# The first eight depth tiles of every down product as seven block products

## The reference

```python
def swiglu(x, w_gu, w_down):
    g, u = jnp.split(x @ w_gu, 2, axis=-1)
    return (jax.nn.silu(g) * u) @ w_down
...
x = layer_norm_2(DN_ALPHA * x + 0.5 * swiglu(x, ffn_w_gu[layer, 0], ffn_w_down[layer, 0]),
                 ln_g[layer, 0], ln_b[layer, 0])
```

## Time and profile before

| | |
|---|---|
| median of 3 runs | 2902.07 us (2901.93 to 2903.99) |
| profiled execution, its own time | 2903.62 us |
| its span, first to last instruction | 2901.8 us |
| TensorE busy | 2857.2 us, 98% of the span |
| DVE / ACT busy | 1707.7 us / 1269.3 us |
| mean granted clock of TensorE | 0.998 |

### The profile page before, as it was taken

One profiled execution on the slowest core, in us unless ns is written; L12 is line 12 of the kernel. 1 busy time (PEld: TensorE's weight loads), 2 busy tenths in 40 slices (PEclk: granted clock), 3 DMA queues, 4 the chain that ended last, 5 costly groups with the idle time before them and its releaser, 6 DMA issues.

```text
span 2901.8 us, 43274 instructions
## 1 busy us (share of the span) xinstructions
PE 2857.2 (98%) x18236; PEld 2507.2 (86%) x18236; DVE 1707.7 (59%) x2268; ACT 1269.3 (44%) x2082; POOL 101.5 (3%) x153
## 2 busy tenths in 40 slices
PE   8999999999999999999999999999999999999998
PEld 6888888778888699998868999898998886799987
DVE  4464342343333778862676988257884458698843
ACT  3324333454434345542473555134553248545531
POOL 1000000001000000000100000010000011000000
PEclk9999999999999999999999999999999999999999
DMA  6432232222222232333302233243333340123232
GB/s 200 141 105 88 102 102 87 88 67 81 80 88 80 71 102 93 112 117 107 100 16 88 91 113 117 91 129 131 108 97 116 79 110 1 59 88 117 88 116 73
DMA packets 186274, 278.67 MB, mean 96 GB/s; under 512 B 29595, under 2 KB 127051, under 8 KB 185953
## 3 DMA queue, kind: packets, MB, share of 16 engines
q1 hardware_dynamic: 177040, 247.17, 26.4%
q0 software_dynamic: 9040, 28.73, 3.1%
HBM read 271.56 MB, written 4.25 MB: 95 GB/s over the span
## 4 chain that ended last, share of the span: by engine, by line
PE 88%; DVE 7%; issue 2%; DMA 1%; ACT 1%; POOL 0%; SPq 0%; POOLq 0%; DVEq 0%; ACTq 0%
PE bank L673 25%; PE bank L675 25%; PE bank L674 25%; PE bank L811 2%; PE bank L899 1%; PE bank L867 1%; PE bank L883 1%; PE bank L831 1%; PE bank L820 1%; PE bank L684 1%; PE bank L687 1%; PE bank L686 1%; PE bank L792 1%; DMA raw<-in_ffn_w_gu 1%; PE bank L1049 0%
## 5 line engine op out<-in xcount | busy, mean ns | idle before, releaser
L1932 DVE TENSOR_TENSOR w_low<-raw,w_high 128x2048 fp32r<-128x2048 f32 (+2 forms) x131 | 293.7, 2242 | 663.3 <-ACT w_high L1463 657.0
L1463 ACT ACTIVATE w_high<-raw 128x2048 fp32r<-128x2048 f32 (+2 forms) x131 | 245.3, 1873 | 527.5 <-PE bank L675 525.6
L673 PE MATMUL bank<-xt_high,w_high 128*128 128x512 f32 (+1 forms) x1128 | 407.2, 361 | 1.3 <-DVE w_low L1932 0.8
L675 PE MATMUL bank<-xt_high,w_low 128*128 128x512 f32 (+1 forms) x1128 | 399.1, 354 | 0.0
L674 PE MATMUL bank<-xt_low,w_high 128*128 128x512 f32 (+1 forms) x1128 | 398.5, 353 | 0.0
L673 PE MATMUL bank<-w_high,hidden_high 128*128 128x512 f32 x640 | 249.3, 390 | 0.0
L675 PE MATMUL bank<-w_high,hidden_low 128*128 128x512 f32 x640 | 249.0, 389 | 0.0
L674 PE MATMUL bank<-w_low,hidden_high 128*128 128x512 f32 x640 | 249.0, 389 | 0.0
L673 PEld LDWEIGHTS bank<-xt_high,w_high 128*128 128x128 f32 x1128 | 212.8, 189 | 38.3 <-issue 9.6
L675 PEld LDWEIGHTS bank<-xt_high,w_low 128*128 128x128 f32 x1128 | 212.8, 189 | 31.0
L674 PEld LDWEIGHTS bank<-xt_low,w_high 128*128 128x128 f32 x1128 | 213.1, 189 | 27.3
(11 more groups left out here) (447 smaller groups left out, 7096.0 us busy)
## 6 DMA issues: line engine op xcount, KB each, us to landing
raw<-in_ffn_w_gu SPq DMA_DIRECT2D x80, 1024.0 KB, 5.2
raw<-in_ffn_w_down SPq DMA_DIRECT2D x44, 1024.0 KB, 4.9
raw<-in_b_w_in SPq DMA_DIRECT2D x40, 1024.0 KB, 5.1
raw<-in_a_w_in SPq DMA_DIRECT2D x23, 1024.0 KB, 5.1
raw<-in_a_w_out SPq DMA_DIRECT2D x8, 1024.0 KB, 4.9
raw<-in_ffn_w_gu SPq DMA_DIRECT2D x16, 512.0 KB, 5.4
raw<-in_w_out SPq DMA_DIRECT2D x5, 1024.0 KB, 4.9
raw<-in_w_mem_kv SPq DMA_DIRECT2D x4, 1024.0 KB, 5.2
```

Source lines behind the costliest of these rows:

```text
L673: pe.matmul(o, lh, rh, start=start, stop=False, skip_group_check=True)
L675: return pe.matmul(o, ll, rh, start=False, stop=stop, skip_group_check=True)
L1463: act.activation(homes[n][0][:, 0:w], RAW[n % 2][:, 0:w], ACT.Copy).then_inc(sem["w_high_ready"], step("w_high_ready", n))
L1932: dve.tensor_tensor(homes[n][1][:, 0:w], RAW[n % 2][:, 0:w], homes[n][0][:, 0:w].bitcast(F32), ALU.subtract).then_inc(sem["w_low_ready"], ...
```

## The change

With the tokens in two halves, the depth tiles 0 to 7 in two halves of four, and the output columns in two halves of 512, the part of the down product that belongs to the first eight depth tiles is a 2 x 2 by 2 x 2 block product. Before, it is done as four panels with all eight block products. After the change it is done as seven block products, numbered b = 0 to 6, of 24 matmuls of 512 columns each (two token tiles, four depth tiles, three matmuls each). Their left operands are hidden blocks or sums of them, their right operands weight blocks or differences of them:

- `block_sum(1)` to `(4)` on DVE make the token sums, in `SUMS`, three buffers of 4 KB a partition. The first three are made in units 5, 6 and 7, behind n = 2; they are split into parts beside the last unit. The space comes from the scratch of GpSimd's transfers, `dynamic_dma_scratch_size`, which goes from 16 KB to 4 KB.
- The four weight blocks of 512 x 512 are loaded as three panels and a fourth, `CORNER`, that lies where the gains of the layer norms lie; GpSimd's next load of gains waits until the corner has been used. `block_difference(1)` to `(4)` on DVE make the weight differences, in the raw buffers or in `LATE` (where the snapshots of the units lie).
- `block_high(b)` on ACT and `block_low(b)` on DVE split the weight operand of each block product into the same two rings.
- Several block products add up in one bank. Where an intermediate result belongs to an output of its own, `add_partial` on DVE adds it from the bank to the residual rows `X`, and TensorE waits for that (`partial_added`) before it adds the next block product to the same bank.
- The ring's order is now: blocks 0 to 3, the panel of depth tiles 8 and 9, block 4, the panel of 10 and 11, blocks 5 and 6, and the other panels as before.

The core of the diff:

```diff
+        for name, k0, c0 in (("block", 0, 0), ("block", 0, 512), ("down", 8, None), ("block", 4, 0)):
...
+        for k0 in range(10, KF, 2):
+            add(("down", l, i), [(0, 2, D, D, rows(wd, k0, 2, 0, D))])
...
+            def block(b):
+                pe.wait_ge(sem["w_low_ready"], at("w_low_ready", ("block", f, b)))
+                if b == 0:
+                    pe.wait_ge(sem["hidden_split"], at("hidden_split", (f, 0)))
+                if b in (1, 2, 3, 5):
+                    pe.wait_ge(sem["block_sum_split"], at("block_sum_split", (f, {1: 1, 2: 2, 3: 3, 5: 4}[b])))
+                if b == 4:
+                    pe.wait_ge(sem["hidden_split"], at("hidden_split", (f, 3)))
...
+                    if b in (2, 3):
+                        pe.wait_ge(sem["partial_added"], at("partial_added", (f, b - 2, t)))
+                    o = ps[(2 * t, 2 * t + 1, 2 * t, 2 * t, 2 * t + 4, 2 * t + 5, 2 * t)[b]][:]
...
+                act.activation(homes[x][0][:], block_raw(f, b), ACT.Copy).then_inc(sem["w_high_ready"], step("w_high_ready", x))
...
+            block_high(1)
+            block_high(2)
+            hidden_high(4)
+            block_high(3)
+            prepare(ids["down", l, i][0])
+            block_high(4)
+            hidden_high(2)
+            hidden_high(3)
+            hidden_high(5)
+            prepare(ids["down", l, i][1])
+            block_sum_high(4)
+            block_high(5)
+            hidden_high(6)
+            block_high(6)
+            for u in range(7, UNITS):
                 hidden_high(u)
...
+                b, row, cols = ((0, 2, slice(0, 512)), (2, 2, slice(512, 1024)), (3, 0, slice(512, 1024)), (1, 2, slice(512, 1024)))[j]
...
+                    dve.scalar_tensor_tensor(out=x, in0=ps[2 * t + (j == 3)][:], scalar=coef, in1=x, op0=ALU.mult,
+                                             op1=ALU.add).then_inc(sem["partial_added"], step("partial_added", (f, j, t)))
...
+                elif u in (5, 6, 7) and n == 2:
+                    block_sum(u - 4)
+            block_low(1)
+            block_difference(2)
+            add_partial(0)
+            block_low(2)
+            block_difference(3)
+            add_partial(3)
+            block_low(3)
+            add_partial(1)
+            hidden_low(4)
+            prepare(ids["down", l, i][0])
+            add_partial(2)
...
+        pool.wait_ge(sem["w_low_ready"], at("w_low_ready", ("block", (0, 0), 5)))
         gains("l00", *GAINS["l00"])
...
+        nc = bacc.Bacc("TRN2", target_bir_lowering=False, num_devices=1, dynamic_dma_scratch_size=4096)
```

More of the change, by code:

```diff
@@ L35 @@
 FACTORS = 7
+BLOCK_K = 8
 SUM_ORDER = (2, 1, 3, 4)
@@ L242, in build @@
     pt0 = place(2 * KB)
+    sums0 = place(12 * KB)
     rg = place(88 * KB)
@@ L404, in build @@
                for half, g in enumerate(ids["unit", l, i, u])}
-    ring = [g for g in range(len(panels)) if g not in homes and g not in unit_of]
+    block_of = {g: f for f in FFN for g in ids["block", *f]}
+    ring = []
+    for g in range(len(panels)):
+        if g in homes or g in unit_of or g in block_of:
+            continue
+        f = next((f for f in FFN if g in ids["down", *f][:2]), None)
+        if f is None:
+            ring.append(g)
+        elif g == ids["down", *f][0]:
+            ring += [("block", f, 0), ("block", f, 1), ("block", f, 2), ("block", f, 3), g, ("block", f, 4)]
+        else:
+            ring += [g, ("block", f, 5), ("block", f, 6)]
     for n, g in enumerate(ring):
@@ L413, in build @@
     for (l, i), tiles in FFN.items():
-        n = ring.index(ids["down", l, i][0])
+        n = ring.index(("block", (l, i), 0))
         a, b = (n - 1) % 2, n % 2
@@ L418, in build @@
         count = FACTORS * (UNITS - 1)
-        for g, q in zip(ids["down", l, i][:2], (count - 4, count - 2)):
+        for b, q in ((0, count - 4), (1, count - 2)):
+            g = ("block", (l, i), b)
             del freed_by[g]
@@ L440, in build, with block_raw, quarter @@
     DIFF4 = SPARE[0][:, 0:4, 256:512]
+    CORNER = at_off("down_corner", [P, 2048], gb0)
+    LATE = at_off("down_difference", [P, 2048], r0)
+    SUMS = [at_off(f"block_sum{n}", [P, 4, 256], sums0 + 4 * KB * n) for n in range(3)]
+    SUM_OF = {1: SUMS[0], 2: SUMS[1], 3: SUMS[2], 4: SUMS[0]}
+    QUARTER = {1: (0, 256), 2: (0, 0), 3: (4, 0), 4: (4, 256)}
+    def block_raw(f, b):
+        g11, g12, g21 = (RAW[g % 2][:] for g in ids["block", *f])
+        return (g11, g11, LATE[:], g12, g21, CORNER[:], LATE[:])[b]
+    def quarter(x, n):
+        k0, t0 = QUARTER[n]
+        return x[:, k0:k0 + 4, t0:t0 + 256]
     slopes = alibi_slopes(HEADS)
@@ L746, in token, with down @@
             return operands
-        def down(name, kt, hh, hl, ready, free, s):
+        def down(name, kt, hh, hl, ready, free, s, opened=(), behind=None):
             gs = ids[name]
@@ L767, in down @@
                             free(t)
-                        ins = accumulate(g, i, kk, t, i == 0 and kk == 0, False)
+                        ins = accumulate(g, i, kk, t, i == 0 and kk == 0 and t not in opened, False)
                 ins.then_inc(sem["product_done"], step("product_done", ("panel", g)))
+                if behind:
+                    behind(i)
             last = len(gs) - 1
@@ L1160, in free @@
+            for b in range(4):
+                block(b)
             def free(t):
[L1161 to L1164, removed]
+                if t < 2:
+                    pe.wait_ge(sem["partial_added"], at("partial_added", (f, 2, t)))
+                    pe.wait_ge(sem["partial_added"], at("partial_added", (f, 3, t)))
```

192 lines of the change are left out of this document (164 added, 28 removed).

## The result

| | before | after |
|---|---|---|
| median of 19 runs each, us | 2903.2 (2901.9 to 2904.8) | 2907.8 (2904.9 to 2913.4) |
| ratio to before, 95% interval | | 1.0018 (1.0012 to 1.0024) |
| profiled span, us | 2901.8 | 2905.9 |

What follows compares the result with a forecast made beforehand. TensorE, busy 98% of the span, was taken as the bound. Matmuls, waits and scratch gave -21.8 + 4 x 2.86 + 0.5 = -9.8 us, so from the 2902.07 us median 2892.3 us was forecast, range 2882 to 2901 us.

Steps and rivals of the forecast that it cites:

- The matmuls and their waits: In each down product, 24 matmuls fewer save 5.44 us, and TensorE waits 2.86 us at the blocks.
- 0.66, 1.64 and 0.56: Forecast TensorE waits in us at block 2, block 3 and the panel behind block 6, in each down product.
- The queue behind block 3's split: On DVE, `add_partial` for block 2's banks stands behind block 3's split, so TensorE waits 1.64 us at block 3.
- the rival in which the blocks run at the low clock: TensorE's pauses let its clock fall in the blocks, the saving is lost: 2914 us; chance 0.10.
- The prediction's reason: Against a falling clock: attention has pauses at granted clock 1.00; only the last 5.8 us, without any matmul, show 0.59.
- the rival in which the gain is eaten up: Late transfers, a late block 1 and the scratch; 4 to 5.5 us of waiting a product: 2896 to 2903 us; chance 0.23.
- The sums beside the units: DVE's sums in units 5, 6 and 7, 1.3 us each unit, are covered and cost nothing; uncovered 16 us in all.
- The scratch: Behind product (0, 1), a quarter of the scratch may hold GpSimd's position loads: 0.5 us taken.
- the far end: Scratch cost with all four position loads 2.2 us late, less 3.2 us spare: 5.6 us.
- the spare time that is there: Behind (0, 1), DVE ends its part 3.2 us before TensorE starts on the next load, landed at 1961.52.
- Its own sign of error: The prediction is wrong if, among other signs, GpSimd's issues of positions stretch past 1950 us.
- The unit stretches: The spans of the units were to stay at 20.16 us each.

Runs made afterwards that it cites:

- dividing the addition: Changed kernel with position loads issued earlier and block 2's addition in two parts, one ahead of block 3's split, one behind: 2892.2 us, ratio 0.9966.
- 12.0 by itself: Kernel before with only the transfer scratch cut from 16 KB to 4 KB: 2914.3 us, ratio 1.0041.
- buffers exchanged: Changed kernel with position loads issued earlier and the SBUF places of the two raw buffers swapped: 2896.8 us, ratio 0.9979.
- at 12 KB: Kernel before with only the transfer scratch cut from 16 KB to 12 KB: 2902.4 us, ratio 1.0000.
- With 8 KB: Kernel before with only the transfer scratch cut from 16 KB to 8 KB: 2907.8 us, ratio 1.0017.
- positions early: Changed kernel, scratch still 4 KB, with the four position loads issued some 50 us earlier into the place of the block sums: 2896.3 us, ratio 0.9979.

## Why the prediction was wrong

**The matmuls and their waits: right.** 5.44 us less and 2.86 us of waiting a product should have given -10.4 us; the down products are 9.87 us shorter. The waits are 0.40, 1.43 and 0.3 us where 0.66, 1.64 and 0.56 stood, because the trace counts a wait from the end of the last matmul, which is 0.39 us long where the next could start after 0.23; the starts agree to 0.1 us. The queue behind block 3's split, which the prediction named as its cause, was confirmed by dividing the addition.

**The clock: right in the blocks, but not tried elsewhere.** It is 1.00 through the blocks, also behind the pauses of 1.42 to 1.44 us, four in the changed kernel; so the rival in which the blocks run at the low clock is out. The prediction's reason was read off too narrowly: it says that only the last 5.8 us show less, yet the trace of before has 0.50 at 2385.1 to 2388.4, in the same attention, 22 us ahead of the stretch of the earlier trace rows. And behind (0, 1) the clock did fall, behind a wait that the prediction did not have. Of the rival in which the gain is eaten up only "some for the scratch" came true, and at many times its price.

**The sums beside the units: right**, nothing that can be measured.

**The scratch: the step that failed.** The prediction put it between nothing and 5.6 us "at the far end", took 0.5 us, "nearest to the spare time that is there", and it cost 11.3 us (12.0 by itself). Three things were wrong in it. The price of a held issue was taken from the issue's own duration, 1.1 us and as much again; but a held issue waits until a transfer ahead of it has landed, 8.9 us behind a 2 MB load and 3 to 4 us behind each position load. So the far end was no bound. The spare time was read from the wrong deadline: 3.2 us up to the load at 1961.5, though in DVE's queue, between its wait and that point, a panel's split was wanted by TensorE at 1955.1. And the wait was priced by its length: 9.3 us of it brought another 2.3 at the half clock. The prediction asked for the work queued behind a waiting instruction at the blocks, and not here. Its own sign of error, issues of positions past 1950 us, is what the trace shows (1951.07). The Trainium skill (Debugging Trainium Hangs, § 4. Descriptor Overflow) counts too many descriptors for the scratch in SBUF among the causes of a hang; here each transfer fits by itself, and a burst of them only waits, 8.88 us at the longest.

**The unit stretches: a small step that failed.** "The spans of the units stay" left out that DVE had no spare time for the first unit's second panel (it waited 1.06 to 1.31 us for it before). Loads of program moved into its transfer and cost 1.77 + 1.49 us in (0, 1) and (1, 1). That in (1, 0), where the panels start earlier, the 0.73 us have the same cause is not shown: a load stands at some 2 us there in five kernels, but only in three of them (the changed one, with the buffers exchanged, with the addition divided) do the first two panels land late, 6.9 to 8.0 us after their issue for 5.1 to 5.8 elsewhere, and just these three have stretches of 193.6 to 194.6 us, all others 192.9. The 1.65 us that the stage behind (1, 0) gave back are the clock of that stage in the profiled executions; no run ties them to the change. The Trainium skill (DMA: Bandwidth & Descriptors, § Queues, rings and completion order) says that a transfer engine goes round its queues packet by packet and finishes a packet before it changes; the trace agrees as far as it goes, as the load is one packet of 16 KB that takes 1.1 us; which engine took it, the trace doesn't tell.

## What to carry to other kernels

Memory taken from the transfer scratch is paid for where GpSimd issues its largest burst: add up the pieces of that burst first, and price a held issue by the landing of what stands ahead of it, not by its own length. The spare time of a waiting instruction ends at the first thing queued behind it on its engine that somebody else wants. A wait of TensorE can cost more than its length, where the clock falls behind it. A buffer that an optimization frees again later, like the 12 KB of sums here, can take the loads that the optimization made late.

## What was not expected of the hardware

- A full scratch shows in the trace only as idle time of GpSimd that ended at "issue", with no semaphore: 8.88 us at 4 KB and none ahead of a position load at 12 KB, for a load of 2 MB and four position loads of 2048 single elements each. With 4 KB even position loads alone hold each other, each until the one before has landed. With 8 KB the fourth position load waited for the third (landed at 1947.6), though the first two had landed by 1944.0; why is open.
- The granted clock of TensorE fell to 0.50 behind waits of 9.33, 9.80, 10.00 and 2.86 us, and behind two of five waits of 2.6 us; in the blocks it stayed at 1.00 behind all twelve waits of 1.4 us (after the change, positions early, buffers exchanged). It also fell in a stretch that the change doesn't touch, the attention behind (1, 0), in five of the eleven profiled executions.
- TensorE's program is loaded in pieces of 16 KB, one some 14 to 19 us after another in the units (before the change at 1076.4 and 1090.9 us), and each takes about 1.1 us of one of the 16 transfer engines. A second panel that met one became ready 0.5 to 2.8 us later (DVE's wait 1.70 to 3.95 us; 0.97 to 1.31 without, and once 1.83). Why it is at times more than the load's own 1.1 us stays open.
